# Second attention on TensorE: transposes and value products ahead of the next scores in every step

## What is computed

```python
def second_block(x, ...):
    h = rms_norm(x, norm_mix[l]);  proj = h @ w_in[l]
    o_a = nsa_mixer(...)             # 4 heads: compressed (31 keys), selected, window, gated and added
    o_b = dilated_mixer(...)         # 2 heads x 3 groups of dilation 1, 4, 16, merged by softmax weights
    o_c = stick_breaking_mixer(...)  # 6 heads, a = exp(log_beta + suffix sum of log_fail)
    x = x + concat(o_a, o_b, o_c) @ w_out[l]
    h = rms_norm(x, norm_mlp[l])
    x = x + jnp.square(jax.nn.relu(h @ w_up[l])) @ w_down[l]
```

## Time and profile before

| | |
|---|---|
| median of three runs | 1190.66 us (1188.73 to 1191.43) |
| the profiled execution | 1190.29 us, of which the span of the trace is 1188.5 us |
| TensorE matmul busy | 1134.3 us (95% of the span), weight loads 949.6 us (80%) |
| VectorE, ScalarE, GpSimd busy | 637.4, 428.2, 485.4 us (54%, 36%, 41%) |
| second attention | about 523 to 797 us of the span |

### The profile page before, as it was taken

How to read it: one execution, slowest core, us unless ns; L and a number is a source line. 1 busy time by engine, 2 the same in 40 slices (tenths; PEclk the granted TensorE clock), 3 DMA queues, 4 the chain that set the end, 5 groups by cost and what they waited for, 6 DMA issues and landing times.

```text
span 1188.5 us, 16034 instructions
## 1 busy us (share of the span) xinstructions
PE 1134.3 (95%) x5740; PEld 949.6 (80%) x5740; DVE 637.4 (54%) x1155; ACT 428.2 (36%) x864; POOL 485.4 (41%) x489
## 2 busy tenths in 40 slices
PE   6999999999979999999998889899999999999998
PEld 5788888888869877977787779777878888888887
DVE  6869777686567644655686666624641231321321
ACT  5373678253436542135455345423020110110110
POOL 0000000000523325970717322507967776776772
PEclk9999999999989999999999899999999999999999
DMA  6422323314211001330302101202332232323221
GB/s 245 135 75 89 124 71 107 128 50 142 89 36 37 20 18 54 112 101 18 103 22 78 65 19 54 71 2 74 121 102 93 89 106 89 101 93 103 92 88 53
DMA packets 27278, 97.16 MB, mean 82 GB/s; under 512 B 3024, under 2 KB 3408, under 8 KB 27088
## 3 DMA queue, kind: packets, MB, share of 16 engines
q1 hardware_dynamic: 27216, 96.32, 24.5%
HBM read 94.21 MB, written 2.10 MB: 81 GB/s over the span
## 4 chain that ended last, share of the span: by engine, by line
PE 72%; DVE 11%; issue 8%; ACT 6%; POOL 2%; DMA 1%; SPq 0%; POOLq 0%; DVEq 0%; ACTq 0%
PE bank L986 20%; PE bank L988 20%; PE bank L987 20%; PE bank L671 4%; PE bank L706 3%; PE bank L689 2%; DVE arena L1726 1%; POOL wl L473 1%; DVE wl L1675 1%; PE bank L674 1%; ACT wh L1336 1%; DVE yl L1909 1%; DMA x<-x_in 1%; POOL wh L470 1%; DVE arena L2118 0%
## 5 line engine op out<-in xcount | busy, mean ns | idle before, releaser
L469 POOL TENSOR_TENSOR hold<-hold 128x2 f32<-128x2 f32 x117 | 28.7, 246 | 628.2 <-PE bank L988 628.1
L986 PE MATMUL bank<-xh,wh 128*128 128x512 f32 x568 | 227.1, 400 | 11.0 <-DVE xl L1644 9.7
L988 PE MATMUL bank<-xh,wl 128*128 128x512 f32 x568 | 222.4, 392 | 0.0
L987 PE MATMUL bank<-xl,wh 128*128 128x512 f32 x568 | 222.2, 391 | 0.0
L986 PE MATMUL bank<-yh,wh 128*128 128x512 f32 x520 | 205.4, 395 | 9.6 <-POOL wl L473 5.2
L988 PE MATMUL bank<-yh,wl 128*128 128x512 f32 x520 | 204.4, 393 | 0.0
L987 PE MATMUL bank<-yl,wh 128*128 128x512 f32 x520 | 204.3, 393 | 0.0
L473 POOL TENSOR_TENSOR wl<-raw,wh 128x512 fp32r<-128x512 f32 x117 | 170.7, 1459 | 0.0
L472 POOL TENSOR_TENSOR wl<-raw,wh 128x512 fp32r<-128x512 f32 x117 | 157.9, 1350 | 9.8
L986 PEld LDWEIGHTS bank<-xh,wh 128*128 128x128 f32 x568 | 107.5, 189 | 33.6 <-issue 11.3
L988 PEld LDWEIGHTS bank<-xh,wl 128*128 128x128 f32 x568 | 107.2, 189 | 22.8
(11 more groups left out here) (239 smaller groups left out, 1820.7 us busy)
## 6 DMA issues: line engine op xcount, KB each, us to landing
raw<-weight_units SPq DMA_DIRECT2D x173, 512.0 KB, 3.4
x<-x_in SPq DMA_DIRECT2D x4, 512.0 KB, 8.0
out_fm<-x SPq DMA_DIRECT2D x8, 256.0 KB, 2.0
arena<-tables SPq DMA_DIRECT2D x1, 1024.0 KB, 10.0
par<-params SPq DMA_DIRECT2D x1, 166.0 KB, 2.4
arena<-swa_table SPq DMA_DIRECT2D x1, 128.0 KB, 10.8
ident<-identity SPq DMA_DIRECT2D x1, 64.0 KB, 7.8
```

The lines of the kernel that those rows point to most:

```text
L469: pool.tensor_tensor(hold[:], hold[:], hold[:], ALU.add).then_inc(held, 1)
L986: pe.matmul(out, lh, rh, start=start, stop=False)
L987: pe.matmul(out, lh, rl, start=False, stop=False)
L988: return pe.matmul(out, ll, rh, start=False, stop=stop)
```

## The change

In the second attention the flag `late` is set from step 0 on, no longer from step 69 on. The scores that are issued before step 0 (groups 0 to 3) stay where they are, and so does everything from step 69 on and all of the first attention. The instructions are the same, with the same waits. VectorE, ScalarE, GpSimd and the DMA queue have the same rows in the same order.

```diff
@@ -718,7 +718,7 @@
                     mm.then_inc(s["pairT"], 1)
 
                 for i in range(-LOOK - 1, ng + OUT_LAG):
-                    late = a == 2 and i + LOOK + 1 > first_dil
+                    late = a == 2 and i >= 0
                     if 0 <= i + LOOK + 1 < ng and not late:
                         scores(i + LOOK + 1)
                     if 0 <= i < ng:
```

## The result

The changed kernel took 1195.76 us (median of 20 executions, 1188.12 to 1207.44), the kernel before on the same chip 1189.99 us (20 executions, 1187.12 to 1193.50). The ratio is 1.0043, with a 95% interval of 1.0023 to 1.0062: slower, by twice what counts as no change. The median hides the shape. Eleven of the 20 executions took 1188.1 to 1196.0 us, with a mean granted clock of 0.981 to 0.988; the other nine took 1202.7 to 1207.4 us, with 0.967 to 0.973. Nothing lies between, and no execution of the kernel before, of 113 in all batches, was above 1200 us. The profiled execution is of the upper group: 1207.3 us, span 1205.5 us.

What follows compares the result with a forecast made beforehand. TensorE was taken as the bound engine, matmuls covering 95% of the span. Lost 2.4 us, gained 1.2, smaller places 0, pitch +0.5 gave +1.7 us on 1190.3: 1192.0 us, range 1187.8 to 1196.0.

Steps and rivals of the forecast that it cites:

- the likeliest case, no change: Whole kernel: time within about 0.2% of the median, 1188.3 to 1193.0 us; chance of same 0.52.
- the forecast's own sign of being wrong: Wrong if waits stay and new ones appear at L671, L689 or L706, or clock is below 1 in another 10 us.
- the first rival: Longer idle at step 51 or 55 lets the clock fall once more, costing 4.1 us: 1196.1 us; chance 10%.
- Late copy at step 27: Scores no longer fill time ahead of VectorE's late copy: 0.63 us lost, transposes wait 4.6 us.
- the 0.34 us taken for `mask1`: Step 27: extreme of group 27 starts 0.59 us later, of which 0.34 us reaches the copy; bounds 0 and 0.59.
- Steps 51 and 55: Scores no longer fill time before late copies: 0.63 and 0.62 us lost; waits grow to about 1.5 and 1.3 us.
- third rival: Turn first speeds all copies, so losses at steps 27, 51 and 55 vanish: 1186.6 us; chance 15%.
- Step 31: Turn in front starts ScalarE's copy and evacuation earlier: 0.57 us gained, the item waits less than 0.3 us.
- Step 70: Turn first in step 68 starts VectorE's chain 0.67 us earlier, a gain; idle at step 70's scores falls 1.08 to 0.4.
- the forecast's terms for these steps: Step 48 on: 0.83 and 0.62 us lost at steps 51 and 55, 0.67 gained at step 70: +0.8 us.
- The pitch in the stick steps: Steps 0 to 19: entering 64-row scores from value products costs more, +0.5 us in all, ends -1.8 and +1.6.
- The second rival: Steps 24 to 63: VectorE absorbs none of eight 0.59 us delays, 4.7 us lost, 1196.2 us; chance 17%.

Runs made afterwards that it cites:

- stick_only: New order only in steps 0 to 19, old order from step 20 on, against the kernel before: 1189.76 us, ratio 0.9993.
- late_20_31: New order only in steps 20 to 31, against the kernel before: 1191.29 us, ratio 1.0011.
- late_32_47: New order only in steps 32 to 47, against the kernel before: 1190.17 us, ratio 1.0021.
- late_48_68: New order only in steps 48 to 68, against the kernel before: 1188.28 us, ratio 0.9992.
- after_fill27: The changed kernel with 14 extra products ahead of the transposes of step 27: 1195.71 us, ratio 1.0017 to the kernel before.
- late_20_47: New order only in steps 20 to 47, against the kernel before: 1201.25 us, ratio 1.0041, 7 of 12 executions over 1200 us.
- after_dense41: The changed kernel with 16 extra products behind the scores of step 41: 1195.08 us, ratio 1.0018 to the kernel before.
- short_only: New order only in steps 20 to 68, against the kernel before: 1196.37 us, ratio 1.0070, 2 of 6 executions over 1200 us.

## Why the prediction was right and wrong

**The sum came near, and beside the point.** The median lies inside the range, near its upper end, but the likeliest case, no change, is not what came: it is slower. That the median is inside is luck: with 10 executions in the upper group in place of 9 it would have been about 1199 us. And the forecast's own sign of being wrong, a granted clock below 1 in another stretch of 10 us, came in the profile. Over the 93 executions of the kernel before in the three batches the time falls with the mean granted clock nearly along a straight line: the means are 1195.28 us at 0.979, 1190.54 at 0.985 and 1185.99 at 0.990. The eleven executions of the changed kernel at 0.981 and over lie 1.2 us above that line (standard error 0.2); the forecast was +1.7. But the kernels with a part of the change do not add up to that: by the same line stick_only lies 0.3 us below, late_20_31 on it, late_32_47 0.5 above and late_48_68 0.2 below (standard errors 0.2 to 0.4), together about nothing. So at equal clock the cost is small, and that the sum sized it rightly is not shown. The mean over all 20, 1198.45, is 7.8 us over the mean of the 93, 1190.65. Most of that is clock.

**The step that failed is the first rival, in its chance, its place and its price.** It was given 10%, in steps 51 or 55, for 8.2 us at half speed. The fall came behind step 38, and 0.50 stood for some 30 us, which made 14.0 us of the profiled execution. "Against it: an idle stretch of 1.7 us in 685 to 695 left the clock at 1.00" was the error: it read one execution as a margin, at the very wait where the clock fell in seven of the thirteen later profiles, in the old order too. That wait did not even grow. Before, and after:

```profile
689.67 0.44 PE L986 MATMUL bank<-wh,xh 128*128 128x384 f32 x1 [1.74 <-ACT arena L1531]
```

```profile
691.09 0.44 PE L986 MATMUL bank<-wh,xh 128*128 128x384 f32 x1 [1.52 <-ACT arena L1531]
```

The length of a stretch at half speed was taken from the one stretch there was, 10.2 us. In the changed kernel that one is longer too (0.66 and 0.66 in 655 to 675, against 0.68 and 0.81), which is the +1.3 us of the table.

**Late copy at step 27: half right.** Forecast 4.6 us of wait, measured 4.14, and 4.13 to 4.15 in six more profiles with the new order there. The scores do go behind it, so their 0.63 us are lost. But the transposes start no later (137.90 against 137.97 us from the first scores); the 0.34 us taken for `mask1` was 0, the lower bound. The rows show why. VectorE and GpSimd in the changed kernel:

```profile
651.65 0.69 DVE L882 CUSTOM_DVE_ANT_0 arena<-bank,arena 128x512 f32<-128x512 f32 x1 [4.22 <-PE bank L689]
...
657.02 1.26 POOL L472 TENSOR_TENSOR wl<-raw,wh 128x512 fp32r<-128x512 f32 x1
657.04 1.38 DVE L2076 TENSOR_TENSOR arena<-arena 64x128 f32<-64x128 f32 x1
...
660.00 0.56 DVE L824 COPY arena<-bank 128x384 f32<-128x384 f32 x1
...
660.71 1.09 PE L689 MATMUL bank<-ident,arena 128*128 128x128 f32 x4 [4.14 <-ACT arena L771]
```

`mask1` is 0.77 us later than in the earlier trace rows, 0.57 less the 0.2 us by which this trace is later anyway: the 0.59 foreseen. At the copy only 0.13 us are left (660.00 against 659.87), less than the 0.2. In between, two waits of VectorE before its next copies, 0.34 and 0.36 us, are gone, and its instruction at L2069, held beside GpSimd in both, takes 1.06 us in place of 1.28.

**Steps 51 and 55: wrong in size.** At full clock step 51 waits 1.10 us (forecast 1.5) and step 55 0.21 (forecast 1.3), with 0.39 new at the pair transposes between them. Together 1.7 us where 2.8 were forecast and 1.36 stood before. The third rival, turn first speeds the copies, may have a part of the truth here; the rows do not show it.

**Step 31: right.** Forecast under 0.3 us, measured 0.31, where 0.83 stood in the earlier trace rows:

```profile
676.40 0.44 PE L986 MATMUL bank<-wh,xh 128*128 128x384 f32 x1 [0.31 <-ACT arena L1531]
```

**Step 70: wrong.** Forecast 0.4 us, measured 1.20 where 1.08 stood. Turn first did start VectorE's chain earlier, but from L847 to the extreme before the scores it now takes 5.64 us (747.72 to 753.36), before 4.96 (749.88 to 754.84): 0.49 of the 0.68 us are the one instruction at L925, 0.17 the one at L929. Both stand beside GpSimd's weight split and end with one of its instructions: L470 runs from 749.41 for 1.04 us, L472 from 750.54 for 1.27; before, L925 fell into a gap between GpSimd's instructions. The gain of 0.67 us was given back there. From the item of step 38 to the scores of step 70 late_48_68 takes 66.30 us, the kernel before 65.66: +0.6, where the forecast's terms for these steps come to +0.8. In this profile the sum thus held by errors that cancel, and the 12 executions of late_48_68, 0.2 us below the line, do not show a loss at all.

**The pitch in the stick steps: 0 in place of +0.5.** A step with 512 columns took 2.90 us from its last item product to the next item (552.64 to 555.54), now 2.88:

```profile
552.90 0.40 PE L988 MATMUL bank<-wh,xl 128*128 128x512 f32 x1
553.13 0.60 PE L689 MATMUL bank<-ident,arena 128*128 128x128 f32 x4
553.57 0.78 PE L706 MATMUL bank<-arena 128*128 128x64 f32 x6
554.28 0.50 PE L671 MATMUL bank<-yh 64*128 64x512 f32 x1
...
555.78 0.50 PE L986 MATMUL bank<-wh,xh 128*128 128x512 f32 x1
```

Entering the scores costs 0.12 us more than entering an item from the value products (554.28 - 553.57 = 0.71, against 0.59 before), not the 0.17 taken from transposes; 0.09 is saved where an item no longer precedes scores, and 0.05 where transposes no longer follow them (0.44 to the values, 0.49 before). So the terms cancel, though each of them is there. The rule of the Trainium skill, "TensorE: Matmul & The Clock Gate", section "Part 2: What happens when you issue a matmul", made the order of products free and the sum 0.5 us lower: in sum the trace agrees, term by term it does not.

**The second rival, late scores starve the softmax,** did not come: at full clock no new wait at L689 appears, and stick steps and step 27 start on time.

**What stays open.** Why the low clock behind step 38 can last with the new order, whether it takes the order of both parts or the chip has a hand in it, and why in after_fill27 the clock fell in step 43; why filling the wait of step 27 in the kernel before made the time worse; and how much of the 1.2 us at equal clock belongs to which step. The five executions of late_20_47 at the higher clock lie 1.2 us below the line, not above, so that this term is not settled to a place either. That short work keeps the clock low rests on the counts of after_dense41 alone; products elsewhere in that stretch weren't tried.

## What to carry to other kernels

Where the granted clock has fallen once in the profile, a reorder must be judged by where it can fall next, over many executions: here the waits changed by tenths of a microsecond and the clock cost up to 14. A wait that left the clock at full speed in one execution is no margin, and the length of the last fall is no price for the next: 10.2 us at the lower level in the kernel before, some 34 in the changed one. Before a gain is put down to "this chain starts earlier", look at what runs on GpSimd beside VectorE's part of it.

## What the hardware showed that was not expected

**One order of work, two outcomes.** short_only and the changed kernel have the same work around step 38 and the same fall to 0.87 in 685 to 695. In one execution 0.96 follows, in the other 0.50 three times over, with TensorE busy 10.00 of 10 us throughout. Being busy did not bring the clock back in these steps.

**A VectorE instruction takes four times as long or more beside GpSimd, or does not, and the starts differ by 0.02 us.** The instruction at L2076 (64x128, part of the GELU of the compression) takes 1.38 us where GpSimd's L472 started 0.02 us ahead of it, as in the rows of step 27 above. In late_32_47, whose code is the kernel before up to step 31, it started 0.01 us ahead of a GpSimd instruction:

```profile
657.02 0.28 DVE L2076 TENSOR_TENSOR arena<-arena 64x128 f32<-64x128 f32 x1
...
657.03 1.20 POOL L470 TENSOR_SCALAR wh<-raw 128x1024 fp32r<-128x1024 f32 x1
...
659.37 0.63 PE L689 MATMUL bank<-ident,arena 128*128 128x128 f32 x4 [1.15 <-ACT arena L771]
```

It took 0.28 us. The instruction at L2069 was short there as well, 0.18 us, where the kernel before has 1.28, and the transposes of step 27 waited 1.15 us, not 3.68. The two together are 2.2 of the 2.5 us. So the longest wait of the earlier trace rows is in the main such holds of VectorE, and its length differs from one execution to the next. The Trainium skill, "SBUF — State Buffer", section "SBUF: two separate sides", says that VectorE and GpSimd share a pair of ports as an exclusive lock, which a VectorE instruction with two inputs in SBUF takes against a GpSimd instruction that reads SBUF, and that whoever starts first keeps it for the whole instruction. L2076 is such an instruction, and with that both pairs of rows agree. The recorded starts do not settle every case: at L2069, with one input tensor, GpSimd started 0.02 us ahead in late_32_47 too, and VectorE was not held:

```profile
654.30 1.33 POOL L472 TENSOR_TENSOR wl<-raw,wh 128x512 fp32r<-128x512 f32 x1
654.32 0.18 DVE L2069 TENSOR_SCALAR gates<-gates 128x48 f32<-128x48 f32 x1
```
